# The projection laid out anew, with the token shift finished in it

## What is computed

```python
proj = xn @ w_in                                   # xn = rmsnorm(x, g_mix); w_in is 1024 x 3328
ret_p, rw_p = proj[..., :1536], proj[..., 1536:]   # retention q, k, v, gate | RWKV r, k, v, lora
prev = jnp.concatenate([s_shift[:, None, :], rw_p[:, :-1]], axis=1)
rw_s = rw_p + (prev - rw_p) * rwkv_mu              # the token shift, on 1792 columns
s_shift_new = rw_p[:, -1]
```

## Time and profile before

| | |
|---|---|
| median of 3 runs | 2185.8 us (2183.77 to 2188.48) |
| the profiled execution, span | 2183.41 us, 2181.6 us |
| busy: PE, DVE, ACT, POOL | 85%, 56%, 38%, 14% |
| mean granted clock of PE | 0.921 |
| projection | 0 to 365 us |
| mixers | 365 to about 880 us |
| the L295 matmuls | 1728, 3 kinds, mean 350 to 354 ns printed |
| DMA, experts' stage | 402 to 404 GB/s |

### The profile page before, as it was taken

How to read it: one execution, slowest core, us unless ns; L and a number is a source line. 1 busy time by engine, 2 the same in 40 slices (tenths; PEclk the granted TensorE clock), 3 DMA queues, 4 the chain that set the end, 5 groups by cost and what they waited for, 6 DMA issues and landing times. The chain is left out here.

```text
span 2181.6 us, 36329 instructions
## 1 busy us (share of the span) xinstructions
PE 1847.1 (85%) x15218; PEld 1559.4 (71%) x15218; DVE 1217.1 (56%) x1285; ACT 835.4 (38%) x923; POOL 305.9 (14%) x262
## 2 busy tenths in 40 slices
PE   5999996687788879589999999854999999999940
PEld 5999996566666667478788888333888888888830
DVE  5200100776788876542333332127899999999926
ACT  4211210332333331340221212003777777777723
POOL 1000000322333323100000000001111111111003
PEclk9999998897999998799999999876999999999975
DMA  4422213417311120855201113526999999999928
GB/s 159 145 79 79 79 49 134 125 60 185 98 65 70 70 62 14 287 213 197 102 29 51 39 59 152 196 85 234 371 404 402 404 403 402 403 402 403 356 102 308
DMA packets 110630, 407.76 MB, mean 187 GB/s; under 512 B 25176, under 2 KB 47960, under 8 KB 82352
## 3 DMA queue, kind: packets, MB, share of 16 engines
q1 hardware_dynamic: 86000, 344.32, 42.6%
q10 hardware_dynamic: 17440, 36.00, 4.4%
q0 software_dynamic: 7072, 25.69, 3.0%
HBM read 345.91 MB, written 68.53 MB: 190 GB/s over the span
## 5 line engine op out<-in xcount | busy, mean ns | idle before, releaser
L2361 DVE TENSOR_TENSOR ex_w_lo<-moe_raw,ex_w_hi 128x2048 fp32r<-128x2048 f32 x192 | 431.2, 2285 | 67.0 <-ACT ex_w_hi L2426 66.9
L2426 ACT CAST ex_w_hi<-moe_raw 128x2048 fp32r<-128x2048 f32 x192 | 364.1, 1913 | 133.3 <-PE banks L2271 90.3
L2271 PE MATMUL banks<-ex_w_hi,ex_x_hi 128*128 128x512 f32 x512 | 208.0, 406 | 10.9 <-issue 6.4
L295 PE MATMUL banks<-pj_w_hi,pj_x_lo 128*128 128x416 f32 x576 | 203.7, 354 | 0.0
L295 PE MATMUL banks<-pj_w_hi,pj_x_hi 128*128 128x416 f32 x576 | 203.3, 353 | 0.1
L2271 PE MATMUL banks<-ex_w_hi,ex_x_lo 128*128 128x512 f32 x512 | 202.1, 395 | 0.0
L2271 PE MATMUL banks<-ex_w_lo,ex_x_hi 128*128 128x512 f32 x512 | 201.5, 394 | 0.0
L295 PE MATMUL banks<-pj_w_lo,pj_x_hi 128*128 128x416 f32 x576 | 201.5, 350 | 0.0
L199 DVE TENSOR_TENSOR pj_w_lo<-pj_w,pj_w_hi 128x3328 fp32r<-128x3328 f32 x8 | 29.0, 3623 | 221.6 <-ACT pj_w_hi L254 221.6
L247 ACT COPY pj_out<-banks 128x416 f32<-128x416 f32 x72 | 36.4, 506 | 253.7 <-PE banks L295 253.7
L2271 PEld LDWEIGHTS banks<-ex_w_hi,ex_x_hi 128*128 128x128 f32 x512 | 97.5, 190 | 42.9 <-issue 21.9
(11 more groups left out here) (375 smaller groups left out, 3823.4 us busy)
## 6 DMA issues: line engine op xcount, KB each, us to landing
moe_raw<-w_e_gate SPq DMA_DIRECT2D x64, 1024.0 KB, 7.7
moe_raw<-w_e_up SPq DMA_DIRECT2D x64, 1024.0 KB, 7.4
moe_raw<-w_e_down SPq DMA_DIRECT2D x64, 1024.0 KB, 7.4
blocks<-ex_y ACTq DMA_DIRECT2D x32, 512.0 KB, 7.7
proj<-pj_out ACTq DMA_DIRECT2D x72, 208.0 KB, 1.9
pj_w<-w_in SPq DMA_DIRECT2D x8, 1664.0 KB, 8.7
mx_pin<-proj SPq DMA_DIRECT2D x8, 1664.0 KB, 7.0
h<-at_h SPq DMA_DIRECT2D x18, 512.0 KB, 2.6
```

Source lines behind the costliest of these rows:

```text
L295: ins = pe.matmul(PS[:, 4 + t % BUFS, 0:W], a[:, t, k, :], b[:, par, k, :], start=k == 0 and n == 0, stop=k == KC - 1 and n == len(pairs) - 1)
L2271: ins = pe.matmul(out, a, b, start=first and i == 0, stop=final and i == 2)
L2361: v.tensor_tensor(w_lo[:, j], raw[:, j], as_f32(w_hi[:, j]), ALU.subtract).then_inc(S_("w_split"), 1)
L2426: act.copy(w_hi[:, j], raw[:, j]).then_inc(S_("w_high"), 1)
```

## The change

The projection is written anew, and the token shift moves into it:

- The columns are seven chunks: 256 (the lora columns), then 512 each for r, k and v of the RWKV part, then 512 three times for the retention. The first four are shifted.
- x comes turned from the host (`xT`), so there are no transposes. It is not scaled before the product; the gain g goes into the weights as they are split, and the row's 1/rms into the eviction. The squares for it are made beside the products.
- Weights lie in `w_in` slice by slice in each partition's row. They are loaded in halves of four slices, and ACT and DVE split them one slice (512 columns) at a time, between the evictions, so PE can start a chunk when its first slice is split.
- Products go round all eight banks. The sample tile holds its high part in 64 columns of the stationary and its low part in the other 64, so it takes two products (16 matmuls), and the two halves are added at the eviction.
- A shifted tile is evicted by DVE in two instructions: pm = p rstd mu, and out = p rstd - pm. SP copies pm one row down into `up`, within SBUF, with one row from the tile before, zeros or the samples' state; POOL adds out + up, and SP stores it. The plain columns are evicted by ACT in one instruction. `out`, `pm` and `up` have three buffers each.
- PE's stream, as the others', is written out without loops.
- In the mixers `prev`, `mu` and the nine shift instructions go, `load` has two transfers and no wait for `r_shifted`, `keys` stands after level 1 and `key_sum` after level 2. The new shift states are stored in the projection.

```diff
+    CHUNKS = [(NRET + 3 * WW, NRW - 3 * WW)] + [(512 * c, 512) for c in (3, 4, 5, 0, 1, 2)]
+    NCH = len(CHUNKS)
+    shifted = lambda c: CHUNKS[c][0] >= NRET
+    W, HALF, BUFS = 512, KC // 2, 3
+    N_RET = sum(not shifted(c) for c in range(NCH))
+    number = lambda c, t: TILES * c + t
...
+                def move_up(c, t):
+                    m, (col, n) = moved(c, t), CHUNKS[c]
+                    b, r = m % BUFS, rows_of(t)
+                    to, cols = S_(f"up{b}"), slice(col - NRET, col - NRET + n)
+                    sp.wait_ge(S_("dve_evicted"), dve_evicted(c, t))
+                    if m >= BUFS:
+                        sp.wait_ge(S_("added"), m - BUFS + 1)
+                    sp.dma_start(up[1:r, b, 0:n], pm[0:r - 1, b, 0:n]).then_inc(to, 16)
+                    if t == 0:
+                        sp.dma_start(up[0:1, b, 0:n], d["zero_row"][:, 0:n]).then_inc(to, 16)
+                    elif t < NT:
+                        sp.dma_start(up[0:1, b, 0:n], pm[P - 1:P, (m - 1) % BUFS, 0:n]).then_inc(to, 16)
+                    else:
+                        sp.wait_ge(to, 32 * (m // BUFS) + 16)
+                        if c == 0:
+                            sp.wait_ge(S_("shift_stored"), 16)
+                        sp.dma_start(up[0:NS:DS, b, 0:n], d["mu_shift"][:, cols]).then_inc(to, 16)
...
+                def store(c, t):
+                    n, (col, width) = number(c, t), CHUNKS[c]
+                    if shifted(c):
+                        sp.wait_ge(S_("added"), moved(c, t) + 1)
+                    elif t < NT:
+                        sp.wait_ge(S_("act_evicted"), act_evicted(c, t))
+                    else:
+                        sp.wait_ge(S_("dve_evicted"), dve_evicted(c, t))
+                    sp.dma_start(d["proj"][t * P:t * P + rows_of(t), col:col + width], out[0:rows_of(t), n % BUFS, 0:width]).then_inc(S_(f"stored{n % BUFS}"), 16)
...
+                load_w(0, 0)
+                load_xT(0)
+                load_w(0, 1)
+                load_xT(1)
+                load_xT(2)
                 load_x(0)
-                sp.dma_start(ident[:], d["ident"][:]).then_inc(S_("consts"), 16)
-                with nc.allow_non_contiguous_dma(reason="a gain by channel"):
-                    sp.dma_start(g[:], d["g_mix"][0].rearrange("(c p) -> p c", p=P)).then_inc(S_("consts"), 16)
-                load_w(0, 0)
+                load_w(1, 0)
+                load_xT(3)
                 load_x(1)
+                load_xT(4)
                 load_w(1, 1)
...
+                for t in range(5, TILES):
+                    load_x(t - 3)
+                    load_xT(t)
+                for t in range(TILES - 3, TILES):
                     load_x(t)
-                with sp.Fori(0, NCH // 2 - 1) as m:
-                    for par in range(2):
-                        sp.wait_ge(S_("w_split"), 2 * m + par + 1)
-                        load_w(2 * m + par + 2, par)
-                sp.wait_ge(S_("zero_stored"), 16)
+                sp.wait_ge(S_("shift_ready"), 1)
+                sp.dma_start(d["mu_shift"].rearrange("b n -> (b n)").rearrange("(p n) -> p n", p=P), ss[:]).then_inc(S_("shift_stored"), 16)
+                last = None
+                for c in range(NCH):
+                    if 1 <= c < NCH - 1:
+                        load_w(c + 1, 0)
+                        load_w(c + 1, 1)
+                    for t in range(TILES):
+                        if shifted(c):
+                            move_up(c, t)
+                        if last:
+                            store(*last)
...
+                def w_low(c, k):
+                    n = CHUNKS[c][1]
+                    v.wait_ge(S_("w_high"), KC * c + k + 1)
+                    src = piece(c, k // HALF)[:, k % HALF * n:(k % HALF + 1) * n]
+                    v.scalar_tensor_tensor(w_lo[:, c % 2, k, 0:n], src, g[:, k:k + 1], as_f32(w_hi[:, c % 2, k, 0:n]), ALU.mult, ALU.subtract).then_inc(S_("w_split"), 1)
...
+                def shares(c, t, src, cols):
+                    r, m, n = rows_of(t), moved(c, t), number(c, t)
+                    rstd, width = st[0:r, t, 2:3], CHUNKS[c][1]
+                    b = m % BUFS
+                    if m >= BUFS:
+                        v.wait_ge(S_(f"up{b}"), 32 * (m // BUFS))
+                        v.wait_ge(S_(f"up{(m + 1) % BUFS}"), 32 * ((m - BUFS + 1) // BUFS + 1))
+                    lk(v.scalar_tensor_tensor(pm[0:r, b, 0:width], src, rstd, mu[0:r, cols], ALU.mult, ALU.mult))
+                    if t >= NT - 1:
+                        q = slice(P - 32, P) if t < NT else slice(0, NS)
+                        if moved(c, t) > NT:
+                            v.wait_ge(S_("raw_stored"), 32 * (m // TILES))
+                        v.tensor_scalar(raw[q, 0:width], src[q], st[q, t, 2:3], None, ALU.mult)
+                    out_free(v, c, t)
+                    v.scalar_tensor_tensor(out[0:r, n % BUFS, 0:width], src, rstd, pm[0:r, b, 0:width], ALU.mult, ALU.subtract).then_inc(S_("dve_evicted"), 1)
...
+                v.wait_ge(S_("g_loaded"), 16)
+                for k in range(HALF):
+                    w_low(0, k)
+                x_low(0)
+                for k in range(HALF, KC):
+                    w_low(0, k)
+                for t in range(1, 4):
+                    x_low(t)
+                v.wait_ge(S_("mu_loaded"), 48)
+                v.tensor_tensor(ss[:], ss[:], mus[:], ALU.mult).then_inc(S_("shift_ready"), 1)
+                x_low(4)
+                evict(0, 0)
+                x_low(5)
+                evict(0, 1)
+                x_low(6)
+                evict(0, 2)
+                x_low(7)
+                for k in range(HALF):
+                    w_low(1, k)
+                x_low(8)
+                for k in range(HALF, KC):
+                    w_low(1, k)
+                for t in range(3, TILES):
+                    evict(0, t)
+                for c in range(1, NCH):
+                    for t in range(TILES):
+                        if shifted(c) or t == NT:
+                            evict(c, t)
+                        if c + 1 < NCH and t < KC:
+                            w_low(c + 1, t)
...
+                        po.wait_ge(S_("dve_evicted"), dve_evicted(c, t))
+                        po.wait_ge(S_(f"up{m % BUFS}"), 32 * (m // BUFS + 1))
+                        po.tensor_tensor(o, o, up[0:r, m % BUFS, 0:width], ALU.add).then_inc(S_("added"), 1)
...
+                def evict(c, t):
+                    n, width = number(c, t), CHUNKS[c][1]
+                    act.wait_ge(S_("projected"), n + 1)
+                    if t == NT:
+                        if c >= 1:
+                            act.wait_ge(S_("dve_evicted"), dve_evicted(c - 1, NT))
+                        act.copy(tmp[:, 0:width], PS[NS:P, n % 8, 0:width]).then_inc(S_("tmp"), 1)
+                    else:
+                        act.wait_ge(S_("rstd"), t + 1)
+                        out_free(act, c, t)
+                        act.activation(out[:, n % BUFS, 0:width], PS[:, n % 8, 0:width], ACT.Copy, scale=st[:, t, 2:3]).then_inc(S_("act_evicted"), 1)
...
+                act.wait_ge(S_("g_loaded"), 16)
+                for k in range(HALF):
+                    w_high(0, k)
+                x_high(0)
+                for k in range(HALF, KC):
+                    w_high(0, k)
+                x_high(1)
+                x_high(2)
+                square(0)
+                x_high(3)
+                square(1)
+                x_high(4)
+                x_high(5)
+                square(2)
+                x_high(6)
+                square(3)
+                x_high(7)
+                for k in range(HALF):
+                    w_high(1, k)
+                x_high(8)
+                for k in range(HALF, KC):
+                    w_high(1, k)
+                for t in range(4, TILES):
+                    square(t)
+                evict(0, NT)
+                for c in range(1, NCH):
+                    for t in range(TILES):
+                        if not shifted(c) or t == NT:
+                            evict(c, t)
+                        if c + 1 < NCH and t < KC:
+                            w_high(c + 1, t)
...
+                        if n >= 8:
+                            b, u = divmod(n - 8, TILES)
+                            if shifted(b) or u == NT:
+                                pe.wait_ge(S_("dve_evicted"), dve_evicted(b, u))
+                            else:
+                                pe.wait_ge(S_("act_evicted"), act_evicted(b, u))
+                        terms = [(x_hi, w_hi), (x_hi, w_lo), (x_lo, w_hi)][0:3 if t < NT else 2]
+                        for k in range(KC):
+                            if t == 0:
+                                pe.wait_ge(S_("w_split"), KC * c + k + 1)
+                            for a, (xs, ws) in enumerate(terms):
```

(73 more changed lines are left out.)

202 lines of the change are left out of this document (90 added, 112 removed).

## The result

The changed kernel takes 2318.0 us (2315.4 to 2319.4), beside 2187.1 (2183.8 to 2190.1) for the kernel before on the same chip: a ratio of 1.060 (1.058 to 1.062). The forecast was 2132, in a range of 2117 to 2155. The change is slower, by 131 us.

A forecast was written before the change was run, and what follows sets the result against it. PE alone was taken to bound the projection, with the mixers' waits read pair by pair. Projection -34.4 and mixers -19.5 summed to -53.9 us, from a median of 2185.8 to 2132, range 2117 to 2155.

The forecast's parts named there:

- copy 0.8 + 1.9: Projection, out buffer's path: issue and landing of the shifted copy (landing 1.9 to 8.7 us), hidden by eight banks, cost 0.
- Rival C: Projection: ring from DVE over SP, copy, POOL and store longer than three tiles; +70 to +100, about 2215 us; chance 0.06.
- Feed and eviction near 50: Projection start: stall of 4 us for loads, 2.5 for DVE's fourth eviction at about 51, 1 for slow matmuls.
- no idle in chunks 2 to 6: Projection, a sign to look for: PE without idle in these chunks, its matmuls 0.227 us apart from the second chunk on.
- Head of the mixers: Start of the mixers: mu and prev loads and nine shift operations go, late constants land sooner; gain 6.5 us (3 to 10).
- key_sum: Mixers: moved ahead of level 3, it delays DVE's multiply there by 1.15 us a pair, and PE waits for it.
- Loads: Mixers: smaller loads let the rotary start sooner; excesses of 7.2, 4.9 and 2.3 us in pairs 7, 1, 5 and 6 go.
- Collision of the rotary with DVE, +4.5: Mixers: POOL's rotary runs beside DVE's first two inverse operations; 0.9 us in five pairs, +4.5 (0 to 10).
- Rival D: Projection: PE's written-out code brings two to four instruction-fetch waits at issue, +8 to +15 us, 2144; chance 0.08.
- Rival B: Projection start fed slowly, loads at 250 to 300 GB/s, mixers' head gaining only 3: 15 to 30 us back, 2153; chance 0.18.
- Rival A: No new stalls: loads at 400 GB/s, evictions in time, no collision; another 12 us gained, 2120; chance 0.17.
- Rival E: The projection doesn't shorten, as its evictions hold each bank: between 2150 and 2186 us; chance 0.04.

The follow-up runs named there:

- run 1: The changed kernel with its shifted copy of 127 rows made in two, 112 and 15 rows (48 and 15 in the sample tile): 2138.8 us, ratio to before 0.980.
- run 4: The changed kernel, copy still 127 rows, with DVE splitting the next chunk's weights behind the evictions of tiles 1 and 2 in shifted chunks: 2298.6 us, ratio 1.052.
- run 5: run 1 with key_sum put back behind level 3 in the mixers, where it stood before: 2128.7 us, ratio to before 0.976.
- run 2: The changed kernel with the shifted copy made in two, 126 rows and 1 (60 and 3 in the sample tile): 2137.3 us, ratio 0.979.
- run 6: run 5 with the third chunk's weight loads issued earlier on SP, among the first chunk's shifted copies: 2131.7 us, ratio to before 0.975.
- run 7: run 6 with the 8 MB fill of zeros moved from pair 2 into projection chunks 4 and 5, in 16 pieces: 2114.9 us, ratio to before 0.967.
- run 3: The changed kernel with the 127-row copy going to the same partitions it comes from, so no token shift is done: 2317.7 us, ratio 1.061.

## Why the prediction was wrong, point by point

**The step that failed** is the term "copy 0.8 + 1.9" of the steady state. The landing of the shifted copy was taken from the store of one projected tile, 128 rows to HBM, and bounded by 8.7. Measured, the transfer alone takes about 10 us, above the upper bound, and from issue to add it is 18.6 us, since the copy before is still on the same DMA engine. The two do not look alike where it matters: 128 rows and 127 rows. In run 1 the large piece lands after 2.5, near the 1.9 taken. The prediction also let the three issues of SP cost nothing; the second held SP for 9 us, and the store behind it.

**Rival C** had the right place (the ring over the copy is longer than its buffers), with 0.06, but not the reason. It gave 8 us a tile, 2215, from landings of 8.7; measured were 10.84 us a tile. Its price was too low since it thought of three landings in a ring of three buffers, where the copies themselves run one behind the other on one DMA engine, which is a rate. That the ring of banks doesn't change it run 4 shows; that a fourth buffer would not either is argued only. Worked out with the measured rate: 24 tiles of 512 columns and 127 rows at 10.84 - 5.45, and 8 narrow ones at 5.75 - 3.0, give 129 + 22 = 151 of the 173 us that lie between the changed kernel's first load of the mixers and run 1's. Most of the other 22 lies at the three changes of chunk: POOL's adds of the sample tile and of the tiles around it are at 190.61, 193.77 and 211.79, two tiles in 21.2 us, where PE needs 5.45 + 3.63, which is 6.7 more than the 5.4 already counted. This working is an estimate: it leaves out what PE gains by running ahead and what run 1 itself loses. "Against it: the stage moves only about 110 GB/s" was the wrong argument: it weighed a mean over the stage against one transfer's own rate.

**With the copy repaired the sum can be tested.** Run 1 takes 2138.8, the forecast was 2132. By profile it gains 46.1 (2181.6 to 2135.5) where 53.9 was summed up: 27.2 of 34.4 in the projection, 20.0 of 19.5 in the mixers, and a loss of 1.1 behind them. The 20.0 is partly luck: 4.5 of it is pair 2 (62.9 us from load to load against 67.4), which was forecast to stay and which differs that much between runs of the same code. The projection of run 1, on PE and SP:

```profile
9.84 0.58 PE L465 MATMUL banks<-pj_w_hi,pj_x_hi 128*128 128x256 f32 x1 [9.84 <-DVE pj_x_lo L295]
...
35.72 0.28 PE L465 MATMUL banks<-pj_w_hi,pj_x_lo 128*128 128x256 f32 x1
...
36.68 0.28 PE L465 MATMUL banks<-pj_w_lo,pj_x_hi 128*128 128x256 f32 x1
...
53.44 0.50 PE L465 MATMUL banks<-pj_w_hi,pj_x_hi 128*128 128x512 f32 x1 [2.08 <-DVE pj_out L311]
...
96.40 0.79 PE L465 MATMUL banks<-pj_w_hi,pj_x_hi 128*128 128x512 f32 x1 [1.78 <-DVE pj_w_lo L289]
...
332.02 0.39 PE L465 MATMUL banks<-pj_w_lo,pj_x_hi 128*128 128x512 f32 x1
...
337.83 0.33 SPq L554 DMA_DIRECT2D mx_pin<-proj  x1
```

- *Stream.* Narrow matmuls come every (36.68 - 35.72)/8 = 0.120 us (0.125 taken), the wide ones every 0.227 as taken. Right.
- *Start.* 9.84 (9 taken, 8 to 13). Right.
- *Feed and eviction near 50.* 1.9 and 0.7 us of waits for x (4 taken), 2.08 for the eviction at 53.44 (2.5 taken, at about 51). Right.
- *Not in the sum:* 1.78 at 96.40 and 1.52 at 99.56, for the split of the third weights, and a few matmuls at a lower clock. Their load stands on SP behind chunk 0's evictions. The step that missed it is "no idle in chunks 2 to 6": it checked the durations on DVE, not when the loads are issued. From 9.84 to 332.02 are 322.2 us for a stream of 309.4, 12.8 over, where 7.5 were taken.
- *End.* 337.83 - 332.02 = 5.8; before it was 3.9, so +1.9 for a term of 1.2.
- *Head of the mixers.* 5.7 us less in the changed kernel, 5.3 in run 1 (6.5 taken).
- *key_sum.* The wait of 1.02 in front of level 3's multiply stood in the profile as forecast. With it moved back the waits for this multiply fell by 8.2 us, the mixers by 5.2: the term of 1.15 a pair was about right as a wait and, as far as two profiles tell, too high as a cost. Which wait takes up the other 3.0 is not shown.
- *Loads.* The rotary waits of PE fell from 9.6 to 1.3 us (the rows of run 5). From the first products to the gate product pair 1 takes 21.63 us in run 1 (26.75 before) and pair 7 22.68 (29.00), 11.4 less together where 12.1 were taken. Right for these two.
- *Collision of the rotary with DVE, +4.5.* It happens, at a little less than its price. In the changed kernel's pair 3, and the second operation in all nine, before and after (ns min/median/max):

```profile
716.54 0.72 POOL L839 TENSOR_TENSOR mx_qk<-mx_pin,mx_rope 128x256 f32<-128x256 f32 x1 [3.45 <-DMA mx_rope<-rope]
716.59 1.22 DVE L692 TENSOR_TENSOR mx_X<-mx_M,mx_lev 128x512 f32<-128x512 f32 x1
717.21 1.17 POOL L840 TENSOR_TENSOR mx_qkt<-mx_pin,mx_rope 128x256 f32<-128x256 f32 x1
717.84 1.09 DVE L693 TENSOR_TENSOR mx_TTT<-mx_X,mx_i 128x512 f32<-128x512 f32 x1
...
L566 DVE TENSOR_TENSOR mx_TTT<-mx_X,mx_i x9: 691/692/693, 414.3 to 845.0; 128x512 f32<-128x512 f32 x9
...
L693 DVE TENSOR_TENSOR mx_TTT<-mx_X,mx_i x9: 691/1090/1094, 554.4 to 977.2; 128x512 f32<-128x512 f32 x9
```

Before, both operations of DVE took 0.69 us in every pair. Now the second takes 1.09 in five of the nine, and in the same five the first takes 0.79 to 1.22: 3.6 us more in five pairs, where 0.9 each, 4.5, were taken. POOL's operations are stretched as well, 1.17 in place of 0.72. PE's waits for `TTT` are 16.9 us in the changed kernel and 15.9 in run 1 against 13.9 before, but 14.1 in run 5, where DVE loses 2.2 in four pairs; so the cost to PE is between 0.2 and 3.0 us. The 1.75 of the earlier trace rows was too dear a neighbour. The higher term of 7.2, from the rule of the Trainium skill (SBUF — State Buffer, "Reading the diagram") that the shared ports are held for a whole instruction, is further off: the most that an operation of DVE lost in this kernel is 0.53, not 0.72. That each side waits for the other the trace shows; whether for a whole instruction it doesn't.

- *Rival D*, fetching of code in the projection: PE has no wait at issue there, in any run. Pair 2 kept its waits until the fill was taken away. *Rival B*, a slow feed: 2.6 us of waits for x against the 15 to 30 given. *Rival A*: not reached, 2138.8 against 2120. *Rival E*: not so, the projection ran at PE's pace in runs 1, 2, 5, 6 and 7.

What stays open: the mixers with the same code take 508.6 us in the changed kernel, 506.8 in run 3, 500.7 in run 4 and 500.0 in runs 1 and 2. Pair 2 with its waits at issue (62.5 to 69.1 us from load to load) is a part of it: 6.2 of the 8.6 us between the changed kernel and run 1, but only 3.6 of the 8.6 between it and run 2.

## What to carry to other kernels

Price a transfer from a row with the same number of rows on the partition side, not the same number of bytes; if no such row exists, look at what divides that number before bounding it. A shift by one row makes 128 into 127, a prime, and cutting the copy in two (112 + 15, or 126 + 1) costs one more issue and gave back 179 us here. And follow a wait to the last idle engine: PE's wait named the weight split, which took 0.74 us; only DVE, a step further back, was waiting for the thing that had a rate. And count a wait's instances in order before reading a duration from it: POOL's waits of 9.6 us looked like the time of one copy, which took 18.6 from its issue.

## What the runs showed of the hardware

- Copies of 127 rows of 2 KB within SBUF ran at 25 to 27 GB/s, about 10 us each, with 0.07 of the sixteen DMA engines' time; two of them at a time meant 18.6 to 19.2 us from issue to the add. In 112 + 15 rows the large piece landed in 2.5.
- A 256 KB store beside such copies landed after 9.1 us instead of 2.3: in the one looked at, fifteen of its sixteen completions came by 2.5 us and the last after 8.9.
- The engine that issues is held too: with such copies under way, SP needed up to 9.8 us (8.76 in the row shown) to issue one row more.
- Beside a fill of 8 MB in one transfer PE waited for its instructions three or four times in pair 2, 8.7 to 12.9 us together, up to 5.0 each; the same bytes in 16 pieces beside a steady stream of matmuls cost nothing that shows.
- POOL beside DVE stretched both: a POOL operation from 0.72 to 1.17 us, the DVE operations from 0.69 to 1.09 and up to 1.22.
